# Encoder layer on one core: two decay buffers and another step order in front of the experts, and a fourth place for their down matrices

## The reference, cut to what matters

```
h = rms_norm(x, norm_mix); z, xbc, dt, q, k, v, u = split(h @ w_in)
mix = concat(ssd(z, silu(conv4(xbc)), softplus(dt)),    # Mamba-2, both directions, chunks of 128
             neighbourhood_attention(q, k, v),          # 4 heads of 64 on an 8 x 64 grid
             pooled(u)) @ w_out
x = x + mix
x = x + softmax(q_n k_n^T) v @ w_xo                     # 4 heads of 128 over 256 memory tokens
h = rms_norm(x, norm_ffn)
g = argmax(h @ w_group + b); two best of the 8 experts of g; gates = softmax(two) * softmax(g)
x = x + sum over the two: gate * ((silu(h @ w_gate[e]) * (h @ w_up[e])) @ w_down[e])   # 32 experts, 1024 x 256
```

## Time and profile before

| | |
|---|---|
| median of 3 runs | 1178.75 us (1177.96 to 1183.33) |
| profiled execution | 1180.71 us, span 1178.7 us |
| mean granted clock of PE | 0.939 of 2.4 GHz |
| busy: PE, DVE, ACT, POOL | 1017.5, 784.9, 466.0, 301.5 us |
| moved | 197.4 MB, mean 167 GB/s |

### The profile page before, as it was taken

How to read it: one execution, slowest core, us unless ns; L and a number is a source line. 1 busy time by engine, 2 the same in 40 slices (tenths; PEclk the granted TensorE clock), 3 DMA queues, 4 the chain that set the end, 5 groups by cost and what they waited for, 6 DMA issues and landing times.

```text
span 1178.7 us, 13976 instructions
## 1 busy us (share of the span) xinstructions
PE 1017.5 (86%) x5029; PEld 808.7 (69%) x5029; DVE 784.9 (67%) x1251; ACT 466.0 (40%) x849; POOL 301.5 (26%) x346
## 2 busy tenths in 40 slices
PE   4898798998898999999979999667999888888983
PEld 3676586767677778788867888555776666666661
DVE  5437776777677677862355676457987777778771
ACT  5123343323234323421234343224665564655640
POOL 2223314221341222200111111004342232343322
PEclk9899999897898989899989999867999999999997
DMA  6132223121132523325110113734899998998962
GB/s 227 46 108 63 81 96 113 46 79 56 47 102 68 169 81 126 108 66 193 57 57 18 54 54 134 285 135 156 343 375 349 349 367 333 362 351 345 363 247 89
DMA packets 63396, 197.40 MB, mean 167 GB/s; under 512 B 16416, under 2 KB 22976, under 8 KB 50912
## 3 DMA queue, kind: packets, MB, share of 16 engines
q1 hardware_dynamic: 43344, 152.73, 35.6%
q0 software_dynamic: 18688, 39.52, 9.4%
q10 hardware_dynamic: 1296, 4.26, 0.9%
HBM read 190.16 MB, written 37.75 MB: 193 GB/s over the span
## 4 chain that ended last, share of the span: by engine, by line
PE 40%; DVE 15%; DMA 11%; issue 10%; ACT 7%; POOL 3%; ACTq 0%; DVEq 0%; POOLq 0%
DMA edr<-w_e_down 10%; PE bank L943 6%; PE bank L944 6%; PE bank L945 6%; DVE egl L1727 3%; PE gu_ps L943 2%; PE gu_ps L945 2%; PE gu_ps L944 2%; PE y_ps L1324 2%; PE bank L1128 2%; PE bank L1010 2%; ACT ghi L1394 1%; PE xg_ps L1289 1%; ACT dec L1570 1%; ACT prob L1588 1%
## 5 line engine op out<-in xcount | busy, mean ns | idle before, releaser
L943 PE MATMUL bank<-Wh,hTh 128*128 128x512 f32 x384 | 160.6, 418 | 7.9 <-issue 6.7
L944 PE MATMUL bank<-Wl,hTh 128*128 128x512 f32 x384 | 155.1, 404 | 0.0
L945 PE MATMUL bank<-Wh,hTl 128*128 128x512 f32 x384 | 154.5, 402 | 0.0
L1727 DVE TENSOR_TENSOR egl<-egr,ghi 128x2048 fp32r<-128x2048 f32 x64 | 143.9, 2288 | 14.9 <-ACT ghi L1394 14.9
L1394 ACT ACTIVATE ghi<-egr 128x2048 fp32r<-128x2048 f32 x64 | 119.5, 1930 | 0.0
L943 PE MATMUL gu_ps<-ghi,xgH 128*128 128x512 f32 x256 | 103.8, 406 | 1.4 <-DVE xgL L2092 1.4
L945 PE MATMUL gu_ps<-ghi,xgL 128*128 128x512 f32 x256 | 101.0, 395 | 0.0
L944 PE MATMUL gu_ps<-egl,xgH 128*128 128x512 f32 x256 | 100.7, 393 | 0.0
L943 PEld LDWEIGHTS bank<-Wh,hTh 128*128 128x128 f32 x384 | 76.2, 198 | 25.0 <-issue 7.4
L1394 ACT ACTIVATE dhi<-edr 128x1024 fp32r<-128x1024 f32 x32 | 33.9, 1060 | 136.1 <-DMA edr<-w_e_down 120.3
L945 PEld LDWEIGHTS bank<-Wh,hTl 128*128 128x128 f32 x384 | 75.4, 196 | 16.8
(11 more groups left out here) (325 smaller groups left out, 2249.0 us busy)
## 6 DMA issues: line engine op xcount, KB each, us to landing
egr<-w_e_gate SPq DMA_DIRECT2D x32, 1024.0 KB, 17.9
egr<-w_e_up SPq DMA_DIRECT2D x32, 1024.0 KB, 21.1
edr<-w_e_down SPq DMA_DIRECT2D x32, 1024.0 KB, 14.5
raw<-w_in SPq DMA_DIRECT2D x50, 256.0 KB, 3.0
xn<-w_in SPq DMA_DIRECT2D x22, 256.0 KB, 3.0
x_sb<-x_prompt SPq DMA_DIRECT2D x8, 512.0 KB, 6.0
partial_rows<-x_sb ACTq DMA_DIRECT2D x8, 512.0 KB, 2.6
ffn_rows<-xn_ffn POOLq DMA_DIRECT2D x8, 512.0 KB, 2.9
```

What stands on the lines that cost most here:

```text
L943: pe.matmul(dst, ah, bh, start=first, stop=False)
L944: pe.matmul(dst, ah, bl, start=False, stop=False)
L945: return pe.matmul(dst, al, bh, start=False, stop=last)
L1727: tt(egl[n % 4][:, a, :, :], egr[n % 4][:, a, :, :], ghi[n % 2][:, a, :, :].bitcast(F32), ALU.subtract)\
```

## The change

1. **Start.** `hT` of tiles 1 and 2 come between the weight quarters, that of tile 3 behind hn1 of tile 0. PE's wait for the derived constants moves from step `init` to `("dtp", 0)`.
2. **Conv.** The first operation of a conv tile (times the middle tap, plus bias) goes from DVE to ACT. Its tanh and last product are a step of their own, `act`, a place later. `na1_0` comes right behind `u_0`; the second half of `dtv` is the step `dtw`; `dt` and `sback_3` come earlier.
3. **SSD.** `dec1`, a second decay buffer, lies over `prob`. `sdec_1` is ahead of `sy_0`; from then on the order is sy_c, sdec_c+2, yn_c, sout_c. `xdt` and `yn` are steps of their own.
4. **Cross attention and routing.** `hT_ffn` transposes x itself; the gain is multiplied once into the router's weights, and 1/rms comes into the logits. `topk` stands behind the router of its tile and ahead of `xo`; the normalised next tile and its transposes stand directly behind `xo`.
5. **Experts.** `edr` has four places (the fourth where dhi1 was; dhi1 is half as large now and lies beside dhi0). Load n waits for the down product of expert n−4 instead of n−3 (its fourth load for the row values of the routing).

DVE runs 960 operations instead of 969 and PE 3484 instead of 3483.

```diff
         if s == 0:
             tl += [("norm", "mix", 0), ("w", U_QK, 0), ("norm", "mix", 1), ("w", U_QK, 1), ("hT", "mix", 0),
-                   ("norm", "mix", 2), ("w", U_QK, 2), ("norm", "mix", 3), ("w", U_QK, 3)]
-            tl += [("hT", "mix", i) for i in range(1, TPS)]
+                   ("norm", "mix", 2), ("w", U_QK, 2), ("hT", "mix", 1), ("norm", "mix", 3), ("w", U_QK, 3),
+                   ("hT", "mix", 2)]
...
 def ssd_groups(s):
-    dec, y, out = ([(kind, s, c) for c in range(TPS)] for kind in ("sdec", "sy", "sout"))
-    back = [[("sback", s, 1), dec[0]]]
-    return back + [[y[0]], [dec[1], out[0]], [y[1]], [dec[2], out[1]], [y[2]], [dec[3], out[2]], [y[3]], [out[3]]]
+    dec, x, y, yn, out = ([(kind, s, c) for c in range(TPS)] for kind in ("sdec", "xdt", "sy", "yn", "sout"))
+    groups = [[("sback", s, 1), dec[0], x[0]], [dec[1]]]
+    for c in range(TPS):
+        groups.append([y[c]] + x[c + 1:c + 2])
+        groups.append(dec[c + 2:c + 3] + [yn[c], out[c]])
+    return groups
...
+        ranked = on(i - 2, ("rank", i - 2), ("slots", i - 2))
+        tl += on(i + 2, ("hT", "xa", i + 2)) + [("xs2", i)] + on(i + 1, ("hn3", "xq", i + 1))
...
+        tl += ranked + on(i - 1, ("norm", "ffn", i - 1))
...
+        tl += on(i - 1, ("router", i - 1), ("topk", i - 1)) + [("xo", i)] + on(i + 3, ("norm", "xa", i + 3))
...
+        decays = [dec, nc.alloc_sbuf_tensor_at("dec1", [P, 2, SSD_H, P], F32, offset=at["prob"])]
...
-                if kind == "init":
+                if step == ("dtp", 0):
                     pe.wait_ge(const_ld, 16 * N_CONST)
                     pe.wait_ge(init, N_INIT)
...
+                    act.activation(cacc[:, k % 2, :], pb(step)[:, :], ACT.Identity, scale=cwh[:, m, 1:2],
+                                   bias=cbh[:, m:m + 1]).then_inc(conv_in, 1)
...
-                    link(ts(acc, b[:, :], cwh[:, m, 1:2], cbh[:, m:m + 1], ALU.mult, ALU.add))
+                    dve.wait_ge(conv_in, k + 1)
...
+                    if step == ("norm", "ffn", 0):
+                        tt(router_w[:, :, :], router_w[:, :, :], per_head(g_ffn, NL), ALU.mult).then_inc(router_g, 1)
...
-                    tt(logits[:, i, :], pb(step)[:, 0:NL], router_b[:, :], ALU.add).then_inc(is_free(step), 1)
+                    stt(logits[:, i, :], pb(step)[:, 0:NL], rs[:, k:k + 1], router_b[:, :], ALU.mult, ALU.add)
...
+                elif n == 3:
+                    sp.wait_ge(vals_full, 1)
                 else:
-                    sp.wait_ge(d_used, n - 2)
-                load_piece(expert(n), edr[n % 3], 2, ed_ld[n % 3])
+                    sp.wait_ge(d_used, n - 3)
+                load_piece(expert(n), edr[n % 4], 2, ed_ld[n % 4])
```

More of the change, by code:

```diff
@@ L103, in timeline @@
         z, norm, h_t = [("z", "z", i) for i in tiles], [("norm", st, i) for i in nxt], [("hT", st, i) for i in nxt]
[L104 to L109, removed]
+        act = [("act", s, m) for m in range(6)]
+        mixed([[u[0], na1[0]], [conv[4]], [act[4], conv[5], conv_t[4]] + (ssd_groups(s - 1)[-1] if s else []),
+               [act[5], na2[0], u_t[0], u[1], nav[0]]], quarters(u0 + U_XS))
+        mixed([[na1[1], conv[0]], [act[0], conv[1], conv_t[0], na2[1]]], quarters(u0 + U_Z))
+        tl += [act[1], conv[2], conv_t[1], u_t[1], nav[1], ("dtv", s), act[2], na1[2], conv[3], norm[0], ("dtw", s), act[3],
+               norm[1]]
+        mixed([[z[0], conv_t[2], h_t[0], na2[2]], [z[1], h_t[1], norm[2], nav[2], na1[3], ("dt", s)],
+               [z[2], h_t[2], conv_t[3], norm[3], na2[3]], [("sback", s, 3), z[3], ("sback", s, 2), nav[3], h_t[3]]],
               quarters(u0 + 5 if s == 0 else U_MK))
-        tl += [("sback", s, 2), ("gain", "xa" if s else "mem")]
+        tl.append(("gain", "xa" if s else "mem"))
     *heads, last = lagged("mk", range(4))
@@ L126, in timeline @@
     xo = quarters(U_XO)
[L127 to L131, removed]
+    tl += [("gain", "ffn"), ("hn1", "xq", 0), ("hn2", "xq", 0), ("out", "out", TPS + 3, 1), ("hn3", "xq", 0),
+           ("hT", "xa", 1), ("norm", "xa", 2), xo[0], xo[1], ("xs1", 0), ("xsn", 0), ("hn1", "xq", 1), ("hn2", "xq", 1),
+           xo[2], xo[3]]
@@ L132, in on @@
+    for i in range(NT):
         def on(j, *steps):
             return list(steps) if 0 <= j < NT else []
-        routed = on(i - 2, ("topk", i - 2))
         ranked = on(i - 2, ("rank", i - 2), ("slots", i - 2))
[L137 to L153, removed]
+        tl += on(i + 2, ("hT", "xa", i + 2)) + [("xs2", i)] + on(i + 1, ("hn3", "xq", i + 1))
+        if i == NT - 1:
+            tl += [("hT", "ffn", i - 1)]
+        tl += [("xav", i)] + on(i + 1, ("xs1", i + 1))
+        if i < NT - 1:
+            tl += on(i - 1, ("hT", "ffn", i - 1)) + [("xsn", i + 1)] + on(i + 2, ("hn1", "xq", i + 2), ("hn2", "xq", i + 2))
+        tl += ranked + on(i - 1, ("norm", "ffn", i - 1))
+        if i == NT - 1:
+            tl.append(("pre", 0))
+        tl += on(i - 1, ("router", i - 1), ("topk", i - 1)) + [("xo", i)] + on(i + 3, ("norm", "xa", i + 3))
@@ L154, in timeline @@
+    i = NT - 1
+    tl += [("norm", "ffn", i), ("hT", "ffn", i), ("rank", i - 1), ("slots", i - 1), ("router", i), ("pre", 1), ("topk", i),
+           ("rank", i), ("slots", i)]
     return tl + [("place",)]
@@ L560, in encoder_layer @@
         eg_ld = [[sem(f"eg_ld{i}{a}") for a in range(2)] for i in range(4)]
[L561 removed]
+        ed_ld = [sem(f"ed_ld{i}") for i in range(4)]
         ghi_done = sem("ghi_done")
@@ L1821, in _ @@
                     ins.then_inc(conv_sum, 1)
+                elif kind == "act":
+                    m, k = step[2], nth("conv", *step[1:])
                     dve.wait_ge(conv_th, k + 1)
@@ L2031, in _ @@
                         dve.wait_ge(ssd_st[SEQS - 1], 16 * TPS)
-                    tt(logits[:, i, :], pb(step)[:, 0:NL], router_b[:, :], ALU.add).then_inc(is_free(step), 1)
+                    k = nth("norm", "ffn", i)
+                    stt(logits[:, i, :], pb(step)[:, 0:NL], rs[:, k:k + 1], router_b[:, :], ALU.mult, ALU.add)\
+                        .then_inc(is_free(step), 1)
                 elif kind == "topk":
@@ L2316, in _ @@
                                 .then_inc(router_ld, 16)
-                elif kind == "hT" and step[1] == "ffn":
-                    i = step[2]
+                elif kind == "router":
+                    i = step[1]
                     pool.wait_ge(xn_done, 1 + nth("norm", "ffn", i))
```

103 lines of the change are left out of this document (64 added, 39 removed).

## The result

The changed kernel takes 1231.51 us (median of 4 runs, 1229.92 to 1233.39) against 1179.03 before: ratio 1.0448, 95% interval 1.0418 to 1.0478, slower by 4.5%. The forecast was 1170 in a range of 1143 to 1190. Spans of the profiled runs: 1178.7 and 1227.9.

What follows compares the result with a forecast made beforehand. PE, slowed by waits in its own queue, bounds the kernel to about 797 us, transfers the expert loop from about 825; −11 −7 −3 +6 +7 +24 −16 −9 = −9 gives 1170 us, range 1143 to 1190.

Steps and rivals of the forecast that it cites:

- Start, −11: Kernel start: PE's wait for constants moves a tile later, saving 8.7 us of waiting and 2.7 of half-speed clock.
- Conv stages, −7 and −3: Conv stages of both sequences: fewer PE waits and clock gaps save 10 us, 7 of it in the first sequence.
- SSD, +6 and +7: SSD stages of the two sequences: waits for dec go, later yn brings longer waits; 6 and 7 us lost after clock.
- Rival 3: SSD stages: the waits for yn and sout don't come, giving −15 instead of +13, total 1142 us; chance 0.15.
- Rival 1: Cross attention gaps and sout waits: slower clock after the new gaps costs more, total 1191 us; chance 0.18.
- Cross attention, +24: Cross-attention loop: DVE's longer queue before the next transposes makes PE wait, 17 us, plus 8 of clock; bounds +8 and +36.
- tail, −16: End of the routing, 740–797 us: 11 us less idle and 5 less from a faster clock; bounds −8 and −20.
- the clock term: Cross attention: five new gaps bring a slower clock, between 0 and 20 us, taken as 8.
- Fourth place, −9: Expert loop, bound by throughput: a fourth down-matrix place only moves loads earlier, saving 9 us; bounds 0 and −29.
- the rival with −29: Expert loop: the ring was bound by latency, so the period stays 9.9 us, total 1150; chance 0.12.
- The signs named in the prediction: Expected: earlier second tile, SSD waits for y of 3–8 us, longer cross-attention period, no tail xn_ffn wait, expert periods near 11.3.
- three signs of being wrong: Expert period below 10.5, PE waits for xn under 2 us per iteration, or first 130 us gaining under 8.

Runs made afterwards that it cites:

- e9: Kernel before with the new start alone (transposes between weight quarters, PE's wait for the constants a tile later, gain loaded later); 1168.3 us, ratio 0.9904.
- e1: Changed kernel with the SSD steps alone put back in the order of before; 1182.4 us, ratio 1.0037 to the kernel before.
- e3: Changed kernel with xdt of the next chunk moved behind sdec and yn, yn left where the change put it; 1230.1 us, ratio 1.0448 to the kernel before.
- e10: e1 with the whole list from the gain of norm_ffn on in the order of before, new data flow kept; 1150.8 us, ratio 0.9772 to the kernel before.
- e5: e1 with topk moved behind xo and the next tile's norm, instead of ahead of xo; 1189.2 us, ratio 1.0066 to the kernel before.
- e8: Kernel before with the fourth place for the down matrices alone; 1179.1 us, ratio 1.0002.
- e11: Kernel before, ring of three, with only half of each down matrix loaded from the fourth expert on (sums wrong, waits and work kept); 1147.9 us, ratio 0.9734.
- e12: e10 with the last two cross-attention tiles and the routing's tail in the changed kernel's order; 1151.1 us, ratio 0.9766 to the kernel before.
- e6: e1 with xs2 moved ahead of hT_xa as in the kernel before, topk left ahead of xo; 1171.7 us, ratio 0.9922 to the kernel before.
- e2: Changed kernel with yn alone moved right behind its sy, ahead of the sdec two chunks on; 1195.7 us, ratio 1.0146 to the kernel before.
- e7: e1 with both the moves of e5 and e6; 1175.0 us, ratio 0.9963 to the kernel before.
- e4: Changed kernel with the moves of e2 and e3 together, second decay buffer kept; 1193.2 us, ratio 1.0125 to the kernel before.

## Why the prediction was wrong, step by step

- **Start, −11: right** (e9: −10.6).
- **Conv stages, −7 and −3: about half of the first, nothing of the second.** At the backward states the changed kernel is 13.5 ahead, 10.3 of it e9's (181.8 there), so 3.2 for the conv stage; kernels with the same list reach this place between 177.2 and 181.3 (last section), so it may be anything from 0.5 to 4.6. The wait in front of the backward states (L1094) is 4.85, where the earlier trace rows have 2.7. The second conv stage takes 123.0 us before, 124.1 in e1 and 128.5 in the changed kernel, where the last sout of the first sequence (a wait of 2.1) lies in it.
- **SSD, +6 and +7: the step that failed.** Between the landmarks it is +27.4 (first SSD and second conv stage, forecast +3) and +16.5 (forecast +7 less 1 for the start of the cross attention); e1 gives 49 for the list. Place and sign were right, the size was not, and two terms made it small. The first is the waits. They were walked with DVE's list alone (8.2, 3.7, 4.9 for yn and 4.6 at a bank); the trace has 11.88, 6.81, 9.05 and 4.6, so 32.3 against 9.2 before: +23 and not +12. In the second sequence the walk had 3.6, 6.4, 3.2 and 2, the trace has 6.8, 9.3, 4.0, 2.4 and 3.4: 25.9 instead of 15.2. Hand-offs that I left out are part of the difference: POOL's xdt and xw ahead of the head norm (3.3 of the first wait, by e3), and, as far as the timelines show, ACT's squares of y ahead of a weight, and the norm's own chain behind the last sdec. The second term is the clock. I let the longer gaps be paid for by before's slow clock: 12 us to be won where no product would run slow, of which I kept 6, and 2 in the second sequence. Net of the new gaps nothing was won: PE's busy time is 86.97 and 87.46 in the first stage, 186.29 and 187.05 in the second. So the first stage is 21.4 of idle time and 0.5 of slower products (forecast +12 and −6), the second 15.7 and 0.8 (forecast +8 and −2), though the wait for the first cross attention's probabilities became 4 shorter (6.75 to 2.80) and not 1. Rival 3, "the waits don't come" (0.15), was on the wrong side, and its support is read from 605 to 740, which is cross attention; from 184 to 290, DVE is busy 79.8 of 106. Rival 1, on the clock, had the right side but made the cross attention its place and the clock its cause.
- **Cross attention, +24, and tail, −16: +20.2 for both.** The period was forecast at 4 us of waits and 1.6 of clock more, and is 4.8 to 5.6 more. From the first transposed probabilities to xav_6 (800.5, before 738.5) it is +31.6, 22.0 of it idle time and 9.6 the slower clock, where the forecast had 17 and 8: the clock term was right, and of the waits were missed the 4.11 us for the router's product with its gain, which is queued in norm_ffn_0 on DVE, and 3.0 ahead of the first xav (649.64). The tail's gain is 11.4 of the 16, and e10 shows that the order of its steps isn't the reason. My reading of the period was also too simple: e5 took topk out of the way of xn and won nothing, while e10 shows what the loop can do.
- **Fourth place, −9: nothing** (e8). That the loop is bound by throughput was right (e11: fewer bytes help, at the same GB/s); the rival with −29 is refuted. What failed is the price of 1 MB moved ahead. In e8 the eleventh gathered tile comes 95.8 us after the first (before 96.8), but the twenty-fourth 245.6 (before 244.6): what is ahead is given back in the periods that follow. Why they are longer stays open. In the Trainium skill, DMA: Bandwidth & Descriptors (Where 436 GB/s comes from) has the limit of about 358 GB/s for loads from HBM; the changed kernel's loop runs at 347 to 368 over 80 to 100 us, within about 3% of it, while the 368 and the 404 in the earlier trace rows show that it is no hard limit. By that rule the fourth place was worth 0, and it was.
- **Sum.** Forecast and measured between the landmarks: start and first conv stage −18 and −13.5; first SSD and second conv stage +3 and +27.4; second SSD stage with the start of the cross attention +6 and +16.5; cross attention and tail +9 and +20.2; ring −9 and −1.4. The misses are 4.5 + 24.4 + 10.5 + 11.2 + 7.6 = 58.2, 35 of them in the SSD. The 35 are 17 of waits, 9 of clock that was not won, and 8.5 in the second conv stage. The other misses go the same way, so nothing balanced them. The range is narrower than its terms: their upper bounds (−4, +4, +25, +36, −8 and 0) add up to 1232. That this is close to the time measured is luck, for the SSD went past its +25 by itself. The signs named in the prediction were no help either: all came (the waits for y with up to 11.9 instead of 8), and none of the three signs of being wrong did (the ring's period is 11.4, the longer waits for xn are 3.63, the start gained 10.3), because none of them asked for the size of the SSD's waits.

## What to carry to other kernels

Moving a step in a list that several engines walk moves it on every one of them: before pricing a wait, walk all the engines between the two ends (here yn: DVE, but its neighbours' inputs come over ACT and POOL), and look at the step that comes directly behind its producer at the end of the row, where no other work is left to cover it. A second buffer seems to pay only if what it lets run early is not put in front of something that was just in time. In a loop bound by bytes, look for bytes, not for depth; and test a bundle of changes one by one: here a start worth 10.6 us and a data flow worth about 16 were hidden under an order of the SSD that cost 49 and one of the cross attention that cost 32 (e1 against e10).

## What was not expected of the hardware

The same wait can cost the clock or not. e10 and e12 have the same list up to the second half of the routing, and PE waits 3.2 us in both at the same place, 1 us apart. The wait in e10:

```profile
108.00 0.66 PE L1069 MATMUL bank<-ident,x_sb 128*128 128x128 f32 x4 [3.21 <-DVE x_sb L1852]
```

the window around it in e10 (busy PE, clock, DMA share, GB/s):

```profile
100.00:130.00 30.00, 26.79 (x139) 1.00 0.25 79
```

the wait in e12:

```profile
109.01 0.90 PE L1066 MATMUL bank<-ident,x_sb 128*128 128x128 f32 x3 [3.19 <-DVE x_sb L1849]
```

and its window:

```profile
100.00:130.00 30.00, 26.81 (x126) 0.89 0.25 79
```

At 1.00 the stretch holds 139 PE instructions, at 0.89 only 126. At the first cross attention e12 is 4.9 us behind e10, though nothing in its list is different up to there. In this window e3, e5 and e6 show the same 0.89 in their profiled executions, e1, e2 and e7 the 1.00 of e10, e4 and the changed kernel 0.94, all with the same list up to there and the same wait of 3.2. They reach the backward states between 177.2 and 181.3 us. So two orders that differ by 4 or 5 us at a landmark can't be told apart by one profiled execution of each, and a price per gap is a mean at best: what decides whether the level falls behind a given wait these runs leave open.
